# Gate products of the second block: half pieces, and two of the three branches' gates beside S5

## The chip, the cores and the metric

The kernel runs on one core of a Trainium2 chip. The metric is the device time of one execution in microseconds, the median of several runs. The core has five engines with a queue of instructions each: TensorE (PE in the profile), VectorE (DVE), ScalarE (ACT), GpSimd (POOL) and SyncE (SP, which here only starts transfers). Everything is float32.

## The reference, cut to what matters

The program computes two blocks in a row on x of 256 tokens by 1024. The change lies in the mixer of the second block. It projects its input with one wide matrix, runs three branches on parts of the projection (RWKV, attention, S5), and adds the branches up under gates:

```
def hybrid_mixer(x, w_in, ...):
    proj = x @ w_in
    y_a = rwkv7_mixer(proj[..., :OFF_MOBA], ...)
    y_b = moba_attention(heads(q), heads(k), heads(v))          # q, k, v: proj[..., OFF_MOBA:OFF_SSM]
    y_c = s5_mixer(proj[..., OFF_SSM:OFF_GATE], ...)
    gates = jax.nn.sigmoid(proj[..., OFF_GATE:] + gate_b).reshape(Bsz, L, N_BRANCHES, D_MODEL)
    merged = (gates[..., 0, :] * (y_a @ w_up_rwkv)
              + gates[..., 1, :] * (y_b @ w_up_moba)
              + gates[..., 2, :] * (y_c @ w_up_ssm))
    return merged @ w_out
```

D_MODEL is 1024, so the gates are a product of x with 1024 x 3072 weights, 1024 columns for each branch. The RWKV scan is y_t = S_t r_t with S_t = S_(t-1) (diag(w_t) + a_t b_t') + v_t k_t', eight heads of 64. S5 is a complex diagonal recurrence over the 256 tokens in 32 groups of 64 states, then a gelu and a gated linear unit:

```
    y = gelu(Re(C h) + d * u)        # h_t = lam * h_(t-1) + B u_t, complex
    zg = y @ glu_w + glu_b
    return zg[..., :D_SSM] * jax.nn.sigmoid(zg[..., D_SSM:])
```

## The kernel before, in words

**Order by steps.** Each engine has one queue, and its order is written by generators. A generator yields STEP (L28) where another may come in. `weave` (L149) goes round: one step of each generator, in the order given, then again. For the second block TensorE and ScalarE weave three generators (L3645, L3661): the RWKV branch, the "side" branches (input projections, attention, S5) and `gates_ahead`; VectorE weaves the first two (L3678). In this text a round is one turn of the weave, counted from 0; in a round an engine issues first the step of RWKV, then that of the side, then that of the gates. The rounds of the engines are not synchronised; semaphores make an engine wait where it needs another's result, and whatever stands behind in its queue waits with it.

**What the rounds hold on TensorE.** Rounds 0 to 12 are the 13 units of the input projection. RWKV's scan goes in two halves of 128 tokens, rounds 13 to 42 and 43 to 72, each of them: four transposes (rounds 13 to 16, 43 to 46), the products G and N1 of two heads a round (17 to 20, 47 to 50), a round of VectorE alone in which it makes the "first powers" (21, 51), then powers and partial inverses of the matrices of all heads (n0, p, Z, X, M: 22 to 30, 52 to 60), AK, G12, and R2 with Y0 (31 to 33, 61 to 63), four rounds of step and gain (34 to 37, 64 to 67), four of the chain over chunks (38 to 41, 68 to 71), and y (42, 72). After it come RWKV's normalisation and its up product. On the side, rounds 13 to 26 are attention, 27 and 28 its up product (`add_branch_tensor`, branch 1), 29 and 30 the input of S5, 33 its transposes. S5 then has 8 parts: `in` of part p + 1 in round 36 + 3p, `out` of part p in round 37 + 3p; rounds 59 and 60 are its gated unit.

**The gates.** One piece is 256 of the columns: 1 MB of weights in a slot of the ring of four slots (`WeightRing`, L111; SyncE loads piece n + 4 once piece n is used), and 32 matmuls of 128x128 by 256 columns into one bank (`product_cols`, L272, called by `gates_tensor`, L2095). Then `gates_scalar` (L2107) applies bias and sigmoid in two instructions. A branch has four pieces. `gates_ahead` (L3109) does branch 1 (attention) in rounds 13 to 16, one piece a round, and branch 0 (RWKV) in rounds 17, 20, 23 and 26. Its bank is bank 7 alone. Branch 2 (S5) is not ahead: `side_branches_tensor` (L3062) does its four pieces in rounds 61 to 64, after S5, and its up product in rounds 65 and 66.

**S5 on the other engines.** For part p VectorE turns the inputs by the angles ("a", L3000 to L3007) in round 34 + 3p, scans in 35 + 3p and turns back ("h", L3019 to L3024) in 36 + 3p. It needs the sine and cosine of the part: GpSimd reduces the angle (L2800, L2802), and ScalarE computes both in round 34 + 3p (`s5_sincos_scalar`, L2891: four instructions, L2894 to L2899). The functions of ScalarE lie in tables; where the next function is in another one, ScalarE loads it (ACT_TABLE_LOAD).

**Memory.** `rwkv_memory` (L2156) gives RWKV its tiles: among them b and k, which TensorE last reads for G and N1 of the second half of the scan (round 50), and bend and kend. The gates of S5 have a tile of their own in the memory of S5.

Of the kernel before, what the change touches and what calls it, by code (L numbers as in the profile page):

```python
# [15 lines left out]
P = 128  # L16
SEQ = 256
TT = SEQ // P
D = 1024
KT = D // P  # L20
# [7 lines left out]
STEP = "step"  # L28
# [1848 lines left out]
HEADS = 8  # L1877
# [215 lines left out]


def gates_tensor(c, s, pe, banks, branch, spaces=0):  # L2095
    for n in range(4):
        name = "gates", branch, n
        c.ring.next(name, s.pieces["gate"][branch][n])
        yield from c.ring.wait_ge(pe, name)
        bank = yield from banks.take(pe, *name)  # L2100
        product_cols(pe, bank, c.hT, c.ring.view(name), KT).then_inc(*pe.mark(*name))
        pe.also("used", *name)
        for _ in range(1 + spaces):
            yield STEP


def gates_scalar(c, s, act, banks, branch, gates, spaces=0):  # L2107
    for n in range(4):
        yield from act.wait_ge("gates", branch, n)
        src = as_cols(banks.of("gates", branch, n))  # L2110
        for j in range(2):
            f = 8 * branch + 2 * n + j
            ins = act.e.activation(gates[:, 2 * n + j, :], src[:, j, :], ACT.Sigmoid, bias=s.v["gate_b_2"][:, f:f + 1])  # L2113
        ins.then_inc(*act.mark("read", "gates", branch, n))
        for _ in range(1 + spaces):
            yield STEP
# [39 lines left out]
def rwkv_memory(s, mem):  # L2156
    s.rwkv_gates = mem.new("rwkv_gates", 8, SEQ)
    s.gates_at = mem.at - 8 * SEQ
    s.rw_yT = mem.new("rw_yT", 4, SEQ)
    s.rw_gate, s.bonus = mem.new("rw_gate", 4, SEQ), mem.new("rw_bonus", 4, SEQ)  # L2160
    s.AR = mem.new("rw_AR", 4, TT, 2 * P)
    s.b, s.k, s.bend, s.kend = (mem.new(f"rw_{name}", 4, SEQ) for name in ("b", "k", "bend", "kend"))
    s.bk_at = mem.at - 16 * SEQ
    s.chunk_decay, s.v_cols = mem.new("rw_chunk_decay", 4, N_CHUNK), mem.new("rw_v_cols", 4, SEQ)
    inner = mem.part()
    scan_memory(s, mem)
    s.lora_w, s.g2, s.z = inner.new("rw_lora_w", 512), inner.new("rw_g2", 512), inner.new("rw_z", 14, SEQ + 1)
    s.rw_r, s.rw_k = inner.new("rw_r", 4, SEQ), inner.new("rw_k_in", 4, SEQ)
    s.low, s.gate_in, s.shift_tmp = inner.new("rw_low", SEQ), inner.new("rw_gate_in", SEQ), inner.new("rw_shift", SEQ)
    s.logw, s.icl = inner.new("rw_logw", 4, SEQ), inner.new("rw_icl", 4, SEQ)  # L2170
    s.kk, s.rw_work, s.ka = inner.new("rw_kk", 4, SEQ), inner.new("rw_work", 4, SEQ), inner.new("rw_ka", 4, SEQ)
    s.run = inner.new("rw_run", 4, SEQ)
# [467 lines left out]
def rwkv_output_vector(c, s):  # L2640
    dve, banks, work, yT = c.rw.dve, c.rw_banks, flat_work(s), s.rw_yT
# [26 lines left out]
    dve.wait_own()  # L2668
    dve.e.tensor_tensor(yT, yT, s.rw_gate, MULT).then_inc(*dve.mark("branch", 0))
    yield STEP  # L2670
    yield from add_branch_vector(c, s, dve, banks, 0, 2, s.rwkv_gates, s.b[:, 0:2, :])

# [80 lines left out]
def s5_memory(s, mem):  # L2755
# [11 lines left out]
    s.sincos = [own, [s.chunk_start[:, n * 2 * SEQ:(n + 1) * 2 * SEQ].rearrange("p (j s) -> p j s", j=2) for n in range(2)]]  # L2767
    s.s5_angle = s.distance
    s.glu = [mem.new(f"s5_glu{n}", 4, SEQ) for n in range(2)]
    s.s5_gates, s.s5_tmp = mem.new("s5_gates", 8, SEQ), mem.new("s5_tmp", 2, SEQ)  # L2770


def s5_u_tensor(c, s):
# [288 lines left out]
def side_branches_tensor(c, s):  # L3062
    pe, banks = c.side.pe, c.side_banks
    yield from units_tensor(c, s)
    for h0 in (0, 4):
        yield from moba_tensor(c, s, h0)
    yield from add_branch_tensor(c, s, pe, banks, 1, s.mb_yT)
    yield from meet(c, "tensor", "moba", "side")
    yield from s5_u_tensor(c, s)
    yield from s5_tensor(c, s)  # L3070
    yield from gates_tensor(c, s, pe, banks, 2)
    yield from add_branch_tensor(c, s, pe, banks, 2, s.s5_yT)


def side_branches_scalar(c, s):
    act, banks = c.side.act, c.side_banks
    yield from units_scalar(c, s)
    for h0 in (0, 4):
        yield from moba_scalar(c, s, h0)
    for half in range(2):  # L3080
        yield STEP
    yield from meet(c, "scalar", "moba", "side")
    yield from s5_u_scalar(c, s)
    yield from s5_scalar(c, s)
    yield from act.wait_ge("branch", 2)
    yield from gates_scalar(c, s, act, banks, 2, s.s5_gates)
    for half in range(2):
        yield STEP


def side_branches_vector(c, s):
    dve, banks = c.side.dve, c.side_banks
# [5 lines left out]
    for n in range(2):  # L3098
        yield STEP
    yield from s5_vector(c, s)  # L3100
    for n in range(4):
        yield STEP
    yield from add_branch_vector(c, s, dve, banks, 2, 1, s.s5_gates, s.s5_tmp)


AHEAD_STEPS = 13


def gates_ahead_tensor(c, s):  # L3109
    for _ in range(AHEAD_STEPS):  # L3110
        yield STEP
    for branch, spaces in ((1, 0), (0, 2)):
        yield from gates_tensor(c, s, c.ahead.pe, c.ahead_banks, branch, spaces)


def gates_ahead_scalar(c, s):
    for _ in range(AHEAD_STEPS):
        yield STEP
    for branch, gates, spaces in ((1, s.merged, 0), (0, s.rwkv_gates, 2)):
        yield from gates_scalar(c, s, c.ahead.act, c.ahead_banks, branch, gates, spaces)  # L3120


# [690 lines left out]
```

## Time and profile before

| | us |
|---|---|
| median of 3 runs | 1790.57 |
| the runs | 1790.54, 1790.57, 1796.24 |
| the profiled execution's own time | 1796.08 |
| its span, first to last instruction | 1794.8 |
| TensorE, busy share of the span | 86% |
| VectorE | 56% |
| ScalarE | 43% |
| GpSimd | 13% |
| mean granted TensorE clock | 0.90 |

The span is cut by the page into 40 slices of 44.9 us. The second block's mixer, of which this document speaks, lies from about 860 us to 1395 us. The granted clock is the share of TensorE's full speed: 1.0 is 2.4 GHz and 0.5 is 1.2 GHz, and a value between them is a stretch in which it was at both. A busy share counts an instruction as busy for as long as it took, so at the half clock TensorE looks as busy with half the work.

### The profile page before, as it was taken

What the parts mean: (1) busy time and instruction counts of PE and PEld (TensorE: products, weight loads), DVE (VectorE), ACT (ScalarE), POOL (GpSimd) and SP (SyncE); (2) the same over time, 40 slices, a digit from 0 to 9 for tenths busy, and PEclk for the clock granted to TensorE, in tenths of its full rate; (3) what the DMA queues carried; (4) which work ended last, traced back from release to release, by engine and by line L of the source; (5) the groups of instructions that cost most, each with busy time, mean ns of one, the idle gap of its engine ahead of it and who ended that gap; (6) DMA issues with size and microseconds to landing.
All of it is one profiled execution on the core that took longest, in us unless ns stands there. A gap on an engine that the chain in (4) does not pass through costs nothing. (4 is left out here: it accounts for less than half of the span.)

```text
span 1794.8 us, 21644 instructions
## 1 busy us (share of the span) xinstructions
PE 1541.8 (86%) x8851; PEld 1288.1 (72%) x8851; DVE 1007.2 (56%) x1254; ACT 779.9 (43%) x1137; POOL 226.7 (13%) x337
## 2 busy tenths in 40 slices
PE   2979779997978879998979897788959589999996
PEld 1968669996877769997878786457848466666664
DVE  6557456666564344445473515984153666666665
ACT  3455255445454344444442222323100276666662
POOL 5421100001132000001880001220001000000000
PEclk9897789999887889999999997679969599999998
DMA  9745158776571046554433231001312369999882
GB/s 341 257 180 179 58 187 294 265 256 210 155 263 38 1 165 197 188 189 131 153 110 104 69 106 48 1 0 45 105 41 74 144 234 349 344 339 348 341 313 94
DMA packets 134585, 310.32 MB, mean 173 GB/s; under 512 B 6239, under 2 KB 99766, under 8 KB 114902
## 3 DMA queue, kind: packets, MB, share of 16 engines
q1 hardware_dynamic: 130326, 299.18, 47.1%
q0 software_dynamic: 3584, 8.71, 1.9%
q8 instruction: 70, 1.15, 0.3%
q10 hardware_dynamic: 576, 1.05, 0.2%
q14 instruction: 29, 0.24, 0.0%
HBM read 307.87 MB, written 1.05 MB: 172 GB/s over the span
## 5 line engine op out<-in xcount | busy, mean ns | idle before, releaser
L310 DVE TENSOR_TENSOR mlp_weights_lo<-weights,mlp_weights_hi 128x2048 fp32r<-128x2048 f32 x64 | 146.5, 2291 | 68.4 <-ACT mlp_weights_hi L300 67.5
L251 PE MATMUL bank<-mlp_in_hi,mlp_weights_hi 128*128 128x256 f32 x512 | 147.3, 288 | 10.3 <-DVE mlp_in_lo L694 10.3
L3501 DVE TENSOR_TENSOR expert_pair_lo<-weights,expert_pair_hi 128x2048 fp32r<-128x2048 f32 x53 | 119.9, 2290 | 63.9 <-ACT expert_pair_hi L3492 63.9
L252 PE MATMUL bank<-mlp_in_lo,mlp_weights_hi 128*128 128x256 f32 x512 | 147.0, 287 | 0.0
L253 PE MATMUL bank<-mlp_in_hi,mlp_weights_lo 128*128 128x256 f32 x512 | 147.0, 287 | 0.0
L300 ACT ACTIVATE mlp_weights_hi<-weights 128x2048 fp32r<-128x2048 f32 x64 | 121.9, 1908 | 55.9 <-issue 46.6
L251 PE MATMUL bank<-expert_pair_hi,x_block_hi 128*128 128x512 f32 x280 | 113.9, 407 | 5.2 <-issue 5.2
L253 PE MATMUL bank<-expert_pair_hi,x_block_lo 128*128 128x512 f32 x280 | 110.2, 394 | 0.0
L252 PE MATMUL bank<-expert_pair_lo,x_block_hi 128*128 128x512 f32 x280 | 110.2, 394 | 0.0
L251 PEld LDWEIGHTS bank<-mlp_in_hi,mlp_weights_hi 128*128 128x128 f32 x512 | 100.5, 196 | 12.1 <-issue 11.1
L562 DVE SCALAR_TENSOR_TENSOR ada<-weights,cond,ada 128x2048 f32<-128x2048 f32 x42 | 100.0, 2380 | 2.3 <-DMA weights<-in_w_ada 1.6
L252 PEld LDWEIGHTS bank<-mlp_in_lo,mlp_weights_hi 128*128 128x128 f32 x512 | 100.4, 196 | 1.1
L275 PE MATMUL bank<-hT,weights 128*128 128x256 f32 x448 | 100.0, 381 | 0.7 <-ACT merged L2113 0.6
L253 PEld LDWEIGHTS bank<-mlp_in_hi,mlp_weights_lo 128*128 128x128 f32 x512 | 100.4, 196 | 0.0
L251 PE MATMUL bank<-mlp_weights_hi,hidden_hi 128*128 128x512 f32 x256 | 100.0, 391 | 0.0
L252 PE MATMUL bank<-mlp_weights_lo,hidden_hi 128*128 128x512 f32 x256 | 100.0, 390 | 0.0
L253 PE MATMUL bank<-mlp_weights_hi,hidden_lo 128*128 128x512 f32 x256 | 99.6, 389 | 0.0
L3492 ACT ACTIVATE expert_pair_hi<-weights 128x2048 fp32r<-128x2048 f32 x53 | 99.2, 1907 | 0.0
L275 PEld LDWEIGHTS bank<-hT,weights 128*128 128x128 f32 x448 | 84.0, 190 | 13.4 <-issue 2.2
L1266 DVE TENSOR_TENSOR hidden_lo<-mlp_raw,hidden_hi 128x512 fp32r<-128x512 f32 x32 | 22.1, 692 | 96.8 <-ACT hidden_hi L1245 96.8
L3609 DVE TENSOR_TENSOR y_sorted<-bank,y_sorted 128x512 f32 (+1 forms) x70 | 48.4, 692 | 43.4 <-PE bank L3537 41.5
L1239 ACT ACTIVATE mlp_raw<-bank 128x512 f32<-128x512 f32 x32 | 19.1, 597 | 122.2 <-PE bank L253 122.2
(738 smaller groups left out, 3858.7 us busy)
## 6 DMA issues: line engine op xcount, KB each, us to landing
weights<-in_w_ada SPq DMA_DIRECT2D x48, 1024.0 KB, 5.0
weights<-in_w_in SPq DMA_DIRECT2D x45, 1024.0 KB, 5.1
weights<-in_expert_w_gate SPq DMA_DIRECT2D x35, 1024.0 KB, 4.8
weights<-in_w_up SPq DMA_DIRECT2D x32, 1024.0 KB, 5.5
weights<-in_w_down SPq DMA_DIRECT2D x32, 1024.0 KB, 5.1
weights<-in_expert_w_up SPq DMA_DIRECT2D x18, 1024.0 KB, 6.1
weights<-in_expert_w_down SPq DMA_DIRECT2D x18, 1024.0 KB, 6.7
expert_raw<-in_expert_w_up SPq DMA_DIRECT2D x17, 1024.0 KB, 6.0
```

Source lines behind the costliest of these rows:

```text
L251: pe.e.matmul(out, lhsT[0], rhs[0], start=start, stop=False)
L252: pe.e.matmul(out, lhsT[0], rhs[1], start=False, stop=False)
L253: return pe.e.matmul(out, lhsT[1], rhs[0], start=False, stop=stop)
L275: ins = pe.e.matmul(bank[:, j * SEQ:(j + 1) * SEQ], w[:, k, j * P:(j + 1) * P], xT[:, k, :], start=k == 0, stop=k == tiles - 1)
L300: act.e.activation(self.of(n)[0], ring.view(name), ACT.Copy).then_inc(*act.mark(*self.key, "high", n))
L310: dve.e.tensor_tensor(lo, ring.view(name), hi.bitcast(F32), SUB).then_inc(*dve.mark(*self.key, "low", n))
L562: dve.e.scalar_tensor_tensor(part, ring.view(name), s.cond[:, k:k + 1], part, MULT, ADD).then_inc(*dve.mark(*name))
L1239: act.e.activation(s.raw, as_cols(c.up_banks.of("up", l, n)), ACT.Relu).then_inc(*act.mark("read", "up", l, n))
L1266: dve.e.tensor_tensor(lo, s.raw, hi.bitcast(F32), SUB).then_inc(*dve.mark("hidden low", l, n))
L3492: act.e.activation(pair[0][:, :, i * D_EXPERT:(i + 1) * D_EXPERT], expert_raw(s, kind, n), ACT.Copy).then_inc(*act.mark("expert", "high", ...
L3501: dve.e.tensor_tensor(pair[1][:, :, part], expert_raw(s, kind, n), pair[0][:, :, part].bitcast(F32), SUB).then_inc(*dve.mark("expert", "lo ...
L3609: dve.e.tensor_tensor(part, c.banks[4 + 2 * (n % 2) + half].unsqueeze(1), part, ADD).then_inc(*dve.mark("expert", "added", n, half))
```

## The change

Three things change, besides blank lines. A gate piece on TensorE is two steps of 16 matmuls, with a STEP between them; ScalarE's step for the piece starts with a STEP, so that it stands in the round of the second half. The gates of all three branches are ahead: AHEAD gives for each branch the empty steps before it and the empty steps behind each piece. By the rounds above that is branch 1 in rounds 13 to 20, two rounds a piece without a gap; branch 0 in rounds 35 and 36, 38 and 39, 41 and 42, 44 and 45; and branch 2 in rounds 51 and 52, 54 and 55, 57 and 58, 60 and 61. The sigmoids stand in the second round of each pair, behind the side's step of that round. The four pieces in rounds 61 to 64 of the side generator go, so S5's up product is in rounds 61 and 62 on TensorE and in 60 and 61 on VectorE. And the gates of S5 are written over RWKV's b and k, so ScalarE waits for the last N1 product before them (`"scan", 1, "N1", 7`), and RWKV's up product takes bend, not b, as its work tile.

```diff
--- before.py
+++ after.py
@@ -2093,12 +2093,19 @@
 
 
 def gates_tensor(c, s, pe, banks, branch, spaces=0):
+
     for n in range(4):
         name = "gates", branch, n
         c.ring.next(name, s.pieces["gate"][branch][n])
         yield from c.ring.wait_ge(pe, name)
-        bank = yield from banks.take(pe, *name)
-        product_cols(pe, bank, c.hT, c.ring.view(name), KT).then_inc(*pe.mark(*name))
+        bank, w = (yield from banks.take(pe, *name)), c.ring.view(name)
+        for j in range(2):
+            for k in range(KT):
+                ins = pe.e.matmul(bank[:, j * SEQ:(j + 1) * SEQ], w[:, k, j * P:(j + 1) * P], c.hT[:, k, :], start=k == 0,
+                                  stop=k == KT - 1)
+            if j == 0:
+                yield STEP
+        ins.then_inc(*pe.mark(*name))
         pe.also("used", *name)
         for _ in range(1 + spaces):
             yield STEP
@@ -2106,6 +2113,7 @@
 
 def gates_scalar(c, s, act, banks, branch, gates, spaces=0):
     for n in range(4):
+        yield STEP
         yield from act.wait_ge("gates", branch, n)
         src = as_cols(banks.of("gates", branch, n))
         for j in range(2):
@@ -2159,7 +2167,9 @@
     s.rw_yT = mem.new("rw_yT", 4, SEQ)
     s.rw_gate, s.bonus = mem.new("rw_gate", 4, SEQ), mem.new("rw_bonus", 4, SEQ)
     s.AR = mem.new("rw_AR", 4, TT, 2 * P)
-    s.b, s.k, s.bend, s.kend = (mem.new(f"rw_{name}", 4, SEQ) for name in ("b", "k", "bend", "kend"))
+    bk = mem.new("rw_bk", 8, SEQ)
+    s.b, s.k, s.s5_gates = bk[:, 0:4, :], bk[:, 4:8, :], bk
+    s.bend, s.kend = mem.new("rw_bend", 4, SEQ), mem.new("rw_kend", 4, SEQ)
     s.bk_at = mem.at - 16 * SEQ
     s.chunk_decay, s.v_cols = mem.new("rw_chunk_decay", 4, N_CHUNK), mem.new("rw_v_cols", 4, SEQ)
     inner = mem.part()
@@ -2668,7 +2678,7 @@
     dve.wait_own()
     dve.e.tensor_tensor(yT, yT, s.rw_gate, MULT).then_inc(*dve.mark("branch", 0))
     yield STEP
-    yield from add_branch_vector(c, s, dve, banks, 0, 2, s.rwkv_gates, s.b[:, 0:2, :])
+    yield from add_branch_vector(c, s, dve, banks, 0, 2, s.rwkv_gates, s.bend[:, 0:2, :])
 
 
 
@@ -2767,7 +2777,7 @@
     s.sincos = [own, [s.chunk_start[:, n * 2 * SEQ:(n + 1) * 2 * SEQ].rearrange("p (j s) -> p j s", j=2) for n in range(2)]]
     s.s5_angle = s.distance
     s.glu = [mem.new(f"s5_glu{n}", 4, SEQ) for n in range(2)]
-    s.s5_gates, s.s5_tmp = mem.new("s5_gates", 8, SEQ), mem.new("s5_tmp", 2, SEQ)
+    s.s5_tmp = mem.new("s5_tmp", 2, SEQ)
 
 
 def s5_u_tensor(c, s):
@@ -3068,7 +3078,6 @@
     yield from meet(c, "tensor", "moba", "side")
     yield from s5_u_tensor(c, s)
     yield from s5_tensor(c, s)
-    yield from gates_tensor(c, s, pe, banks, 2)
     yield from add_branch_tensor(c, s, pe, banks, 2, s.s5_yT)
 
 
@@ -3082,8 +3091,6 @@
     yield from meet(c, "scalar", "moba", "side")
     yield from s5_u_scalar(c, s)
     yield from s5_scalar(c, s)
-    yield from act.wait_ge("branch", 2)
-    yield from gates_scalar(c, s, act, banks, 2, s.s5_gates)
     for half in range(2):
         yield STEP
 
@@ -3098,25 +3105,26 @@
     for n in range(2):
         yield STEP
     yield from s5_vector(c, s)
-    for n in range(4):
-        yield STEP
     yield from add_branch_vector(c, s, dve, banks, 2, 1, s.s5_gates, s.s5_tmp)
 
 
-AHEAD_STEPS = 13
+AHEAD = (1, 13, 0), (0, 14, 1), (2, 4, 1)
 
 
 def gates_ahead_tensor(c, s):
-    for _ in range(AHEAD_STEPS):
-        yield STEP
-    for branch, spaces in ((1, 0), (0, 2)):
+    for branch, steps, spaces in AHEAD:
+        for _ in range(steps):
+            yield STEP
         yield from gates_tensor(c, s, c.ahead.pe, c.ahead_banks, branch, spaces)
 
 
 def gates_ahead_scalar(c, s):
-    for _ in range(AHEAD_STEPS):
-        yield STEP
-    for branch, gates, spaces in ((1, s.merged, 0), (0, s.rwkv_gates, 2)):
+
+    for (branch, steps, spaces), gates in zip(AHEAD, (s.merged, s.rwkv_gates, s.s5_gates)):
+        for _ in range(steps):
+            yield STEP
+        if branch == 2:
+            yield from c.ahead.act.wait_ge("scan", 1, "N1", HEADS - 1)
         yield from gates_scalar(c, s, c.ahead.act, c.ahead_banks, branch, gates, spaces)
```

## Rows read from the trace of the kernel before

**Rows 1.** The page, part 2: granted TensorE clock in tenths, 40 slices.

```profile
PEclk9897789999887889999999997679969599999998
```

**Rows 2.** Windows: busy us (and instructions) of each engine, clock, DMA share, GB/s.

```profile
952.20:1051.30 99.10, 90.31 (x536) 79.03 (x537) 35.60 (x77) 32.64 (x69) 0.00 (x0) 0.98 0.23 75
...
1105.30:1171.30 66.00, 52.79 (x410) 33.29 (x409) 52.05 (x84) 22.21 (x42) 19.66 (x12) 0.66 0.00 1
1171.30:1196.40 25.10, 18.05 (x82) 12.26 (x81) 23.43 (x41) 1.67 (x4) 3.19 (x2) 0.77 0.00 1
1196.40:1234.85 38.45, 34.63 (x208) 26.58 (x209) 26.25 (x41) 15.07 (x24) 3.33 (x2) 0.84 0.00 1
...
1253.90:1310.90 57.00, 53.52 (x451) 46.61 (x450) 12.60 (x22) 6.82 (x15) 0.00 (x0) 1.00 0.36 121
```

**Rows 3.** TensorE in order of time, rounds 13 to 26: start us, us, what.

```profile
953.44 7.17 PE L275 MATMUL bank<-hT,weights 128*128 128x256 f32 x32
...
1012.44 2.05 PE L2357 MATMUL bank<-scan_N,scan_PP 128*128 128x128 f32 x16
1017.36 0.98 PE L1307 MATMUL bank<-identity,mb_scores 128*128 128x128 f32 x4 [2.87 <-DVE mb_scores L2742]
1018.13 3.31 PE L2357 MATMUL bank<-scan_PP,scan_N 128*128 128x128 f32 x16
...
1039.78 1.09 PE L1307 MATMUL bank<-identity,mb_scores 128*128 128x128 f32 x8 [3.02 <-DVE mb_scores L2742]
```

**Rows 4.** VectorE in order of time, rounds 20 and 21.

```profile
1004.19 0.69 DVE L2544 TENSOR_TENSOR scan_G<-bank,pair_masks 128x512 f32<-128x512 f32 x1 [0.37 <-PE bank L2387]
...
1011.17 1.22 DVE L2559 TENSOR_TENSOR scan_N<-scan_N,scan_N 128x1024 f32<-128x1024 f32 x1
```

**Rows 5.** Waits from 1100 to 1240 us: who for whom, total us, times, longest.

```profile
DVE s_br L3000 <- ACT s_cos L2899: 11.9, 2, 7.5
...
PE bank L2856 <- DVE s_gi L3024: 11.7, 4, 3.9
```

**Rows 6.** TensorE in order of time, beside S5 (in of parts 1, 4; out of 6).

```profile
1116.14 4.20 PE L2822 MATMUL bank<-s_u,s_bT 32*128 32x256 f32 x8 [1.37 <-DVE s_gi L3001]
...
1159.52 2.31 PE L2822 MATMUL bank<-s_u,s_bT 32*128 32x256 f32 x8
...
1216.97 0.62 PE L2856 MATMUL bank<-s_br,s_cT 128*32 128x256 f32 x2
...
1219.71 2.05 PE L2357 MATMUL bank<-scan_N,scan_PP 128*128 128x128 f32 x16
```

**Rows 7.** ScalarE in order of time: gate, table load, exp; sine and cosine of part 1.

```profile
1012.50 0.84 ACT L2113 ACTIVATE rwkv_gates<-bank,columns 128x256 f32<-128x256 f32 x2 [12.32 <-PE bank L275]
1013.36 1.28 ACT L1294 ACT_TABLE_LOAD   x1
1014.65 0.40 ACT L1294 ACTIVATE mb_scores<-mb_scores,mb_negmax 128x128 f32<-128x128 f32 x1
...
1124.56 0.62 ACT L2894 ACTIVATE chunk_start<-distance 128x512 f32<-128x512 f32 x1
...
1126.39 0.72 ACT L2899 ACTIVATE chunk_start<-chunk_start,ones 128x512 f32<-128x512 f32 x1
```

**Rows 8.** VectorE in order of time: turns of parts 0 and 4, first G of round 47.

```profile
1114.80 0.69 DVE L3000 TENSOR_TENSOR s_br<-bank,s_cos 128x512 f32<-128x512 f32 x1 [7.50 <-ACT s_cos L2899]
...
1166.58 0.68 DVE L3000 TENSOR_TENSOR s_br<-bank,s_cos 128x512 f32<-128x512 f32 x1
...
1172.53 0.69 DVE L2544 TENSOR_TENSOR scan_G<-bank,pair_masks 128x512 f32<-128x512 f32 x1 [1.89 <-PE bank L2387]
```

**Rows 9.** TensorE in order of time: rounds 52, 60 and 68.

```profile
1196.38 3.75 PE L2357 MATMUL bank<-scan_N,scan_PP 128*128 128x128 f32 x16 [6.36 <-DVE scan_N L2559]
...
1243.43 1.80 PE L2357 MATMUL bank<-scan_N,scan_P 128*128 128x128 f32 x14 [1.51 <-ACT scan_N L2364]
...
1310.88 1.80 PE L2471 MATMUL bank<-scan_state,scan_N 128*128 128x64 f32 x8 [1.49 <-DVE scan_N L2595]
```

## The prediction

> **What bounds the kernel now.** I read the clock of the page first, then the windows of the mixer, then each engine in order of time, and the list of waits to see who holds whom.
>
> The clock row [rows 1] shows slices at 6 and 7 in the middle of the second block. The windows [rows 2] say what lies there. From 952 to 1051 us (rounds 13 to 26: attention, the scan's first half, eight gate pieces) TensorE is busy 90 of 99 us at a clock of 0.98, VectorE 36 and ScalarE 33: TensorE sets the pace. From 1105 to 1171 us (rounds 34 to 46: S5's parts 0 to 3) it is the other way round: VectorE is busy 52 of 66 us, TensorE 53, but at a clock of 0.66, so its work would take 52.8 x 0.66 = 35 us at full clock. From 1171 to 1196 us VectorE is busy 23.4 of 25.1. From 1196 to 1235 us TensorE's 34.6 at 0.84 are 29 us of full-clock work in 38.5. From 1254 to 1311 us (rounds 61 to 67) TensorE is busy 53.5 of 57 at 1.00 again, VectorE 12.6, ScalarE 6.8. So TensorE is the limit before S5 and behind it, and has room beside S5: 66 - 35 = 31 us and 38.5 - 29 = 9.5 us, and a wait of 6.36 us at the end of the stretch between [rows 9].
>
> A gate piece takes 7.17 us at full clock, less what overlaps with its neighbours, 7.1 [rows 3], so a branch takes 28.4 and half a piece 3.55.
>
> **The change part by part.**
>
> *Branch 0 leaves rounds 17 to 26.* 4 x 7.1 = 28.4 us of TensorE go, and the halves of branch 1 fill rounds 13 to 20. What do the pieces cover there? Two waits for attention's maps stand in the rows, 2.87 and 3.02 us [rows 3]. I carried rounds 13 to 26 through with the pieces at their new places. The piece of round 20 covers the first powers: VectorE is done with them at 1012.4, which is 8.2 us after it took the first G of round 20 at 1004.2 [rows 4]. After the G of the round and the scores the new order has only a half piece there, 3.55 us in place of 7.1, so TensorE waits about 3.5 us for the powers. The wait of 2.87 shrinks by some 1.9, since the exponentials, too, have only waited for the powers, and ScalarE has no gate and no new table before them (it loaded one, 1.28 us, between gate and exp [rows 7]). The one of 3.02 shrinks by about 1, for the same reason. Sum of the waits: +3.5 - 1.9 - 1 = about +0.5. More waits in a row can let the clock fall: after the wait of 2.87 us the next 16 matmuls took 3.31 us, where 16 of the same form took 2.05 before it [rows 3]. I allow two such falls, about 2 us. Stage: -28.4 + 0.5 + 2 = **-26**. Bounds: -28.4 (waits all hidden), and -14, if half of what goes comes back as waits; VectorE and ScalarE are each busy a third of the stage, so I take the value near the first end.
>
> *Branch 0 goes into rounds 35 to 45.* Eight halves are 28.4 us at full clock; with TensorE's 35 that is 63.4, in a stage of 66. So at full clock it just fits, and the price is what order and clock add. The clock: the stage starts low (in of part 1 takes 4.20 us, that of part 4 takes 2.31 [rows 6]), so the first half piece takes 7.1 and the work beside it also doubles: +5 or so. Then TensorE has no gap left and I expect 1.0, as it is wherever gates run [rows 2]. The order: ScalarE's sigmoid of a piece stands right before sine and cosine of the next part. It waits for the second half, takes 0.84, loads the sine's table 1.28 and computes for 2.55 (1124.56 to 1127.11) [rows 7]: VectorE can start the next part 4.7 us after the half piece ends. For parts 1 to 3 that is no later than TensorE itself comes to the part's out. For part 4 it binds. The last half ends when TensorE has done 35 - 3 (out of part 3, 2.7 us at full clock [rows 6], is behind it) + 28.4 + 5 = 65 us, plus about 3 us of waits for VectorE, which it has today (11.7 us in four waits for S5 [rows 5]); that is 1105.3 + 68 = 1173. Part 4 starts at 1178, against 1166.6 [rows 8]: +11.5. VectorE's next G stood behind a wait of 1.89 us for TensorE [rows 8], which some of it absorbs, or not, if TensorE is late as well. I take **+12**. Bounds: 0 (all in the room of 31 us) and +28.4 (nothing hidden at full clock); beyond it only by the clock, a rival below.
>
> On tables the Trainium skill speaks against this edit: in "ScalarE: Activation LUTs", section "What ACT_TABLE_LOAD costs", a switch of tables costs about 1.28 us for the load and 1.38 more for a drain. By that page the sum would be 1.4 us worse for each of some six parts, 8 us. The rows show the load of 1.28 us begin 0.02 us after the sigmoid and the exponential begin 0.01 us after the load [rows 7], so this trace shows no drain, and the sum has none.
>
> *Rounds 47 to 51.* No piece in them but the first half of branch 2. VectorE is the limit (23.4 of 25.1 us): the 12 us are carried through, neither grown nor made good. The half piece stands in round 51, where TensorE waits 6.36 us for the powers [rows 9], and costs nothing; without that cover it costs 3.55. ScalarE's new wait for the last N1 is for a product a round back. Behind it in its queue stands the evacuation of n0, which comes later anyway.
>
> *Rounds 52 to 68.* Five more halves (branch 2, pieces 0 to 2) come beside parts 5 to 7: 17.75 us with TensorE's 29 make 46.9 in a stage of 38.45: **+8.4**. Here TensorE binds. The sigmoid of piece 2 stands behind ScalarE's evacuation of the gated unit and before that of M, so Z3 waits not 1.51 us [rows 9] but one load and one sigmoid more: **+2**. The last two halves stand in rounds 60 and 61: **+7.1**. The four pieces of rounds 61 to 64 go: **-28.4** (the stage's clock is 1.00). S5's up product moves from rounds 65, 66 to 61, 62 and costs the same; there it covers the evacuation of G12, now about 2 us of wait: **-2**. In rounds 64 to 67 step and gain lose their cover; the wait of 1.49 us behind them [rows 9] stands already, and VectorE's work in the whole stage is 12.6 us [rows 2], so between 0 and a few us can come out there, and I take 0. VectorE's product for S5's up stands in round 60, before its copy of AK, on which G12 waits; but a half piece of 3.55 us lies between on TensorE, longer than the two VectorE instructions and the copy. The clock falls once more, at the half piece and n0 after the powers: +2. Stage: 8.4 + 2 + 7.1 - 28.4 - 2 + 2 = **-11**. Bounds: -21 (the five halves hidden) and +2 (halves at 1.2 GHz).
>
> *What costs nothing.* b, k and bend share the memory of before, so no address conflict or copy is added. The ring's loads keep their number; each still has four pieces of lead, and the DMA share in S5 is 0.00 [rows 2]. Behind round 68 nothing changes.
>
> **Sum.** -26 + 12 - 11 = -25 us against the profiled execution's 1796.1 (span 1794.8 and 1.3 around it): 1771. That execution was at the upper of the values shown; the median is 1790.6, 0.997 of it, so 1771.1 x 0.997 = **1765.7**.
>
> **Rivals.**
>
> *The coupling through ScalarE and VectorE is longer than I think* (chance 0.26, with the case that attention's waits come out in rounds 17 to 26). S5's parts today follow one another on VectorE every (1166.6 - 1114.8) / 4 = 13 us [rows 8]. I have TensorE at 16 us a part; if out, sigmoid, table, sine and turn in series make it 18, four parts cost 20 us, not 12, and three more in the next stage 4 more: -13 in all, 1777.5. The other case has -14 for the first stage: also about 1777. For: 11.9 us of waits for the cosine stand there already, with no gate before it [rows 5]. Against: ScalarE is busy 22 of 66 us.
>
> *The clock stays low beside S5* (0.08): the other side. If the half pieces between S5's narrow matmuls don't raise it, the stage takes 63.4 / clock. At 0.66, as now, that is 96 us, +30, and the next stage 46.9 / 0.84, +17: the sum is -26 + 30 - 11 + 9 = +2, 1792.6. At 0.55 the stage takes 115, +49: 1811. It decides from a clock of about 0.67 in the stage down. For: the clock there is 0.66 with TensorE busy 80% of the time. Against: wherever gate pieces run it is 0.98 to 1.00 [rows 2].
>
> *It doesn't matter* (0.03): the 31 us of room fall short and the 28.4 taken from either side return as waits. It needs both stages wrong at once.
>
> **How the numbers follow.** My forecast has 0.63, its own spread 1757 to 1774. The range goes to the long coupling and a bit beyond, 1753 to 1784. A measurement of this kernel can tell about 0.3% (5 us) from no change. Faster: 0.63 + 0.26 = 0.89; same 0.03; slower 0.08.
>
> **What would show it.** After the change attention's last heads product should end about 26 us earlier, with a wait of some 3.5 us before n0 of the first half. Beside S5's parts 0 to 3 the clock should be above 0.85, the stage 76 to 80 us, and TensorE's waits for S5's turns nearly gone. Sine and cosine of parts 1 to 4 should follow a table load right behind a sigmoid. Rounds 61 to 67 should take about 30 us: today's 57 less four pieces and the wait of 2, plus one half piece. I am wrong if the clock beside S5 stays under 0.7, if VectorE's waits for the cosine grow past 15 us, or if rounds 13 to 26 shorten by less than 20 us.

## The result, and the profile after

| | before | after |
|---|---|---|
| median, us (5 runs each) | 1790.57 | 1782.10 |
| lowest and highest | 1790.46, 1796.24 | 1777.96, 1783.53 |
| after / before, 95% interval | | 0.9943 [0.9929, 0.9956] |
| the profiled execution: time, span | 1796.08, 1794.8 | 1780.62, 1779.4 |
| granted clock, mean | 0.90 | 0.908 |

The change makes the kernel 0.57% faster, 10 us by the ratio, where 25 were forecast. The measured time lies in the range, near its upper end, and by the rival of the long coupling (1777.5), not by the forecast (1765.7).

I cut the second block's mixer by landmarks that both traces have, from the first instruction of round 13 on. "Turn" is VectorE's start on a part of S5, as in [rows 8].

| stretch, us | before | after | difference | forecast |
|---|---|---|---|---|
| round 13 to attention's up product | 100.9 | 73.3 | -27.6 | -26 |
| to the turn of part 0 | 61.7 | 62.4 | +0.7 | 0 |
| to the turn of part 4 | 51.8 | 76.0 | **+24.2** | +12 |
| to n0 of the second half | 29.8 | 31.8 | +2.0 | 0 |
| to the last product of round 68 | 114.5 | 101.7 | -12.8 | -11 |
| to the RWKV branch's up product | 36.4 | 37.7 | +1.3 | 0 |
| sum | 395.0 | 383.0 | -12.1 | -25 |

A forecast of 0 stands where the prediction named no change.

"The last product of round 68" is the group of [rows 9] at 1310.88 us, and a stretch ends where its landmark starts. Four of the terms are near. One is off by 12 us, and it is nearly all of the miss. Round 13 itself starts 2.4 us earlier (at 949.84 in place of 952.23 us), before anything that was changed. The two profiled executions differ by 15.5 us, the ratio of all runs says 10: that of before was the slow end of its runs. So differences below 5 us between executions are read from stages, not from totals.

The windows of the changed kernel answer to [rows 2]: rounds 13 to 26; S5's parts 0 to 3 by TensorE's rounds 34 to 46; rounds 47 to 51; rounds 52 to 60; rounds 61 to 67. The last row goes from the turn of part 0 to that of part 4.

```profile
949.84:1021.25 71.41, 61.17 (x409) 52.70 (x409) 34.88 (x76) 23.71 (x58) 0.00 (x0) 1.00 0.19 60
1075.30:1162.04 86.74, 81.56 (x537) 60.55 (x536) 50.57 (x79) 33.96 (x55) 16.28 (x10) 0.80 0.15 49
1162.04:1193.43 31.39, 25.45 (x98) 17.37 (x97) 27.82 (x47) 3.88 (x8) 6.43 (x4) 0.73 0.00 1
1193.43:1239.85 46.42, 45.70 (x289) 37.83 (x289) 26.64 (x41) 20.60 (x31) 3.22 (x2) 1.00 0.16 47
1260.98:1295.10 34.12, 34.12 (x370) 31.07 (x368) 14.22 (x23) 4.02 (x9) 0.00 (x0) 0.95 0.39 124
...
1085.58:1161.61 76.03, 70.96 (x430) 52.45 (x429) 49.29 (x77) 29.03 (x46) 13.08 (x8) 0.83 0.17 56
```

Beside S5 the clock rose from 0.66 to 0.80, less than the 0.85 I wanted. VectorE's work in the stretch hardly changed (50.6 us, 52.1 before), but the stretch grew by 20.7: VectorE is idle for 36 us of it, where it was for 14. The waits of 1075 to 1193 us say for whom (engine, line, waited for: total us, times, longest). They answer to [rows 5], from VectorE's side:

```profile
DVE s_br L3010 <- ACT s_cos L2909: 13.5, 3, 8.3
DVE s_br L3010 <- ACT chunk_start L2909: 10.3, 2, 5.9
DVE scan_N L2611 <- PE bank L2481: 7.1, 1, 7.1
...
ACT rwkv_gates L2121 <- PE bank L2104: 37.8, 4, 15.1
```

The cosine lies in s_cos and chunk_start by turns. The turns waited 23.8 us for it, 8.3 of them ahead of part 0 (7.5 before, [rows 8]) and 15.5 in the stretch between parts 0 and 4, where before had 0.85. ScalarE itself is idle: it waits 37.8 us for half pieces of TensorE. In order of time on ScalarE, round 39:

```profile
1125.09 0.84 ACT L2121 ACTIVATE rwkv_gates<-bank,columns 128x256 f32<-128x256 f32 x2 [15.06 <-PE bank L2104]
1125.94 1.28 ACT L2904 ACT_TABLE_LOAD   x1
1127.24 0.63 ACT L2904 ACTIVATE s_sin<-distance 128x512 f32<-128x512 f32 x1
...
1129.08 0.72 ACT L2909 ACTIVATE s_cos<-s_cos,ones 128x512 f32<-128x512 f32 x1
```

ScalarE had nothing to do for 15 us, while sine and cosine of part 2 stood in its queue behind a sigmoid that waited for TensorE. GpSimd, which prepares their argument, had been idle since 1113.1 (the window of 1113.10 in the last fence of this document). At 1129.8 us VectorE's turn of part 2 begins, 3.48 us after it could. The same on TensorE, three of the eight half pieces:

```profile
1080.34 4.20 PE L2832 MATMUL bank<-s_u,s_bT 32*128 32x256 f32 x8
1084.60 6.51 PE L2104 MATMUL bank<-hT,weights 128*128 128x256 f32 x16
...
1118.36 6.69 PE L2104 MATMUL bank<-hT,weights 128*128 128x256 f32 x16
...
1129.50 3.67 PE L2104 MATMUL bank<-hT,weights 128*128 128x256 f32 x16
```

A half piece takes 3.67 us at a clock of 1.0 and 6.5 to 6.7 at the low level. The eight take 39.3 us together (6.51, 5.96, 3.67, 6.69, 3.67, 5.41, 3.62, 3.72), where I had 28.4 + 5.

### The profile page after: what moved, and what is told of

Same layout as the page of the kernel before. It is cut to its first block and busy times, and to the rows that moved or that the text cites. A ratio compares the mean times of both kernels' runs of the same rounds, so it can differ in the third digit from the quotient of the medians.

```text
span 1779.4 us, 21643 instructions
## 1 busy us (share of the span) xinstructions
PE 1537.1 (86%) x8851; PEld 1285.2 (72%) x8851; DVE 1010.1 (57%) x1254; ACT 786.7 (44%) x1142; POOL 226.4 (13%) x337
## 5 line engine op out<-in xcount | busy, mean ns | idle before, releaser
L251 PE MATMUL bank<-mlp_in_hi,mlp_weights_hi 128*128 128x256 f32 x512 | 147.4, 288 | 10.3 <-DVE mlp_in_lo L694 10.3
L251 PEld LDWEIGHTS bank<-mlp_in_hi,mlp_weights_hi 128*128 128x128 f32 x512 | 100.5, 196 | 12.1 <-issue 11.1
L2104 PEld LDWEIGHTS bank<-hT,weights 128*128 128x128 f32 x384 | 78.0, 208 | 18.7 <-PE bank L2832 4.2
```

Of the source, the lines that this page charges most:

```text
L251: pe.e.matmul(out, lhsT[0], rhs[0], start=start, stop=False)
L2104: ins = pe.e.matmul(bank[:, j * SEQ:(j + 1) * SEQ], w[:, k, j * P:(j + 1) * P], c.hT[:, k, :], start=k == 0, stop=k == KT - 1)
```

## The experiments

Theory A, from these rows: the order on ScalarE. What stands there ahead of sine and cosine and waits for TensorE holds them; they hold VectorE's turn, and that holds the rest. Theory B: the volume. The half pieces at a low clock are simply too much beside S5; the order matters little. Each experiment is an edit of the changed kernel; the ratios are to the kernel before, run beside it. They were run in three sets, in which the kernel before took 1793.69 us (e1 to e4), 1795.67 (e5 to e8) and 1795.88 (e9 to e12), so the medians of two sets don't compare directly, while the times in the expectations start from the first measurement, with 1790.57. The stretches are the better scale: where nothing differs they agree to 0.1 us (the first is 73.3 us in ten of the traces).

| run | median us | ratio, 95% interval | parts 0 to 4, us | round 13 to up product |
|---|---|---|---|---|
| before | 1793.69 to 1795.88 | 1 | 51.8 | 395.0 |
| changed | 1782.10 | 0.9943 [0.9929, 0.9956] | 76.0 | 383.0 |
| e1_sine_first | 1771.24 | 0.9889 [0.9866, 0.9911] | 71.1 | 376.2 |
| e2_no_table | 1772.76 | 0.9878 [0.9855, 0.9902] | 68.1 | 372.9 |
| e3_branch2_only | 1774.68 | 0.9897 [0.9877, 0.9918] | 51.8 | 376.4 |
| e4_branch0_only | 1789.33 | 0.9984 [0.9967, 1.0001] | 72.8 | 388.0 |
| e5_half_volume | 1772.80 | 0.9876 [0.9858, 0.9894] | 67.2 | 373.5 |
| e6_first_piece_ahead | 1766.65 | 0.9837 [0.9817, 0.9857] | 67.5 | 369.4 |
| e7_branch2_earlier | 1770.04 | 0.9871 [0.9853, 0.9888] | 71.1 | 371.1 |
| e8_places_by_waits | 1752.38 | 0.9767 [0.9748, 0.9785] | 51.7 | 353.2 |
| e9_sines_earlier | 1766.74 | 0.9850 [0.9832, 0.9868] | 64.6 | 369.4 |
| e10_sines_earlier_half_volume | 1756.92 | 0.9790 [0.9772, 0.9809] | 56.9 | 359.3 |
| e11_places_sines_earlier | 1754.84 | 0.9777 [0.9761, 0.9794] | 51.0 | 353.0 |
| e12_whole_pieces | 1790.99 | 0.9977 [0.9965, 0.9989] | 88.7 | 393.5 |

**e1: sine before sigmoid.** ScalarE takes each sigmoid of branch 0 one round later; those of branch 2 keep their rounds.

```
 for _ in range(steps):
->
 for _ in range(steps + (0, 1, -1)[(1, 0, 2).index(branch)]):
```

> ScalarE's sigmoids of branch 0 stand one round later, behind the sine and cosine of the next part; TensorE and VectorE keep their order. In the changed kernel VectorE's parts 0 to 4 of S5 start 19.0 us apart, and it waits 4.4, 3.5, 5.9 and 1.8 us for the cosine of parts 1 to 4. Theory A (the sigmoid in front of the sine holds VectorE, and the low clock comes from the waits that this makes): the four waits go, parts are about 16 us apart, the clock of the stage (rounds 34 to 46) rises from 0.80 to 0.9 or more, time 1770 to 1774 us where the changed kernel has 1782. Theory B (half pieces between narrow products run at the low clock by themselves, and TensorE is what VectorE waits for in the end): the waits for the cosine turn into waits for TensorE's products, parts stay at 18 us or more, the clock at 0.8, time 1779 to 1783.

Measured: 4.9 us of the 24 come back, and the time is in Theory A's range (1771.24), but the parts are 17.8 us apart, near Theory B's 18. VectorE's waits for the cosine of parts 1 to 4 were 4.4, 3.5, 5.9 and 1.8 us and are 2.8, 0, 10.0 and 0: two are gone, and one has grown. ScalarE around the sine of part 3, and the turn behind it:

```profile
1138.03 0.60 ACT L2504 ACTIVATE scan_W<-bank 128x512 f32<-128x512 f32 x1 [18.19 <-PE bank L2390]
1138.64 1.28 ACT L2904 ACT_TABLE_LOAD   x1
```

```profile
1142.53 0.69 DVE L3010 TENSOR_TENSOR s_br<-bank,chunk_start 128x512 f32<-128x512 f32 x1 [10.03 <-ACT chunk_start L2909]
```

The sigmoid is out of the way, but the scan's own evacuation of scan_W stands there too, and waits for transposes that TensorE does behind a half piece. The queue has two such gatekeepers. So this run moved only one, and doesn't decide.

**e2: no table.** The gates of branch 0 are linear (the sigmoid is left out), so ScalarE changes tables less.

```
 ACT.Sigmoid  ->  ACT.Identity if branch == 0 else ACT.Sigmoid
```

> Branch 0's gates are computed without the sigmoid (bias only), so ScalarE loads no table for them and none for the sine behind them; the order is that of the changed kernel. Theory A: only the wait for the half piece counts, of the 4.7 us between it and VectorE's start 1.3 go, so about 4 x 1.3 = 5 us, 1777. Theory B: nothing, 1780 to 1783. Theory C (the tables are the greater part of the miss): 8 us or more, under 1774.

Measured: 7.9 us less between parts 0 and 4 and 1772.8 us, about what I had set for Theory C (8 us or more, under 1774). Four loads lie between a half piece and a turn there, 5.1 us at 1.28; that more came back is for TensorE's side, which is busy 65.8 us in place of 71.0, at a clock of 0.89. 16 us stay, so the loads are a part of the price and not all of it.

**e3, e4: one branch alone.** In e3 branch 0 stands ahead of S5, in rounds 21 to 31; in e4 branch 2 is four whole pieces in rounds 61 to 64 again.

```
 AHEAD = (1, 13, 0), (0, 14, 1), (2, 4, 1)
->
 AHEAD = (1, 13, 0), (0, 0, 1), (2, 18, 1)     # e3
 AHEAD = (1, 13, 0), (0, 14, 1)                # e4, and in the tail:
+    yield from whole_gates_tensor(c, s, pe, banks, 2)
```

> Branch 2's gates stay in rounds 51 to 61 as in the changed kernel, branch 0's go back before S5, as half pieces in rounds 21 and 22, 24 and 25, 27 and 28, 30 and 31. Against the kernel before this is the move of branch 2 alone. By the trace of the changed kernel rounds 52 to 67 give 12.8 us and the first 35 rounds nothing: 1778 to 1780. If the two moves of the change work against each other (branch 0 beside S5 delays the rest), it is better than the changed kernel, if branch 0's move is worth something by itself, worse: Theory A and B both say that branch 0's move gave 27.7 and cost 27.0, so the same as the changed kernel within 3 us.

> Branch 0's gates beside S5 as in the changed kernel, branch 2's as four whole pieces in rounds 61 to 64 as in the kernel before. This is the move of branch 0 alone. By the two traces it gives 27.7 us in rounds 13 to 26 and costs 20.7 in rounds 34 to 46 and 6.3 in rounds 47 to 51: 1790 us, the same as before. Had my forecast been right it would be 1790.6 - 26 + 12 = 1777.

Measured: in e3 S5 is back at 51.8 us, to the tenth what it was; the stretches ahead of it take 82.9 and 72.8 us in place of 73.3 and 62.4, 20.0 more, so by the stages branch 0's move from there into S5 costs 24.2 and saves 20.0. Left ahead of S5, it makes the kernel faster than the change does (0.9897 against 0.9943; the intervals don't meet), where I had expected 1778 to 1780 us, about the same. In e4 the stretch behind n0 takes 113.5 us in place of 101.7: the move of branch 2 is worth 11.8, and I had 11. Branch 0's move alone can't be told from no change (0.9984, an interval that reaches 1): the gain of the change is branch 2's.

**e5: half of the volume.** The RWKV branch's gates sum four of their eight k-tiles; the other half of their products is left out.

```
+ tiles = KT // 2 if branch == 0 else KT
- for k in range(KT):
+ for k in range(tiles):
```

> Every half piece of branch 0 sums over four of the eight tiles of 128 rows only: 8 matmuls in place of 16, same places, same waits, same sigmoids. In the changed kernel VectorE's parts 0 to 4 take 76.0 us (51.8 before). Theory A (the order on ScalarE is what costs): the tables and the order are all there, so of the 24.3 us some 15 or more stay, 1773 to 1776. Theory B (the volume of matmuls beside S5, at a clock that is half the time the low one, makes TensorE late for everything behind it): TensorE has 14 us less at full clock and 20 or more at the clocks seen, so under 10 of the 24.3 us stay, under 1769.

Measured: 14.2 us of work at full clock go, and 8.8 us come back; 15.4 of the 24.2 stay with half of the work. By the volume alone half of the price, 12.1, should have gone with half of the work. 8.8 is less, but not by so much that the volume could be left out. What stays is what I had set for Theory A (15 or more).

**e6, e7: small moves on top of e1.** e6 puts the first piece of branch 0 into rounds 31 and 32, e7 starts branch 2 one round earlier.

```
 (0, 0, 31, 32, 32)          # e6: branch, piece, rounds of its halves, round of the sigmoid
 (2, 4, 1) -> (2, 3, 1)      # e7
```

> As e1_sine_first, but piece 0 of branch 0 is in rounds 31 and 32, in front of the 8 us in which TensorE waits for VectorE to make S5's matrices. Theory B: the piece costs nothing there, and rounds 35 and 36 lose a half piece each that took 6.5 and 3.7 us: parts 0 to 4 take 71.1 - 8 to 10 = 61 to 63 us, time 1763. If the wait of 8 us does not swallow the piece (because ScalarE's table and sigmoid come in the way of S5's start) it is 1768 to 1770.

> As e1_sine_first, but branch 2's pieces start one round earlier, in round 50: the last half piece but one comes between the gated unit's product and Z3, and the sigmoid of piece 2 no longer stands between ScalarE's evacuation of the gated unit and that of M. In the changed kernel TensorE waits 3.66 us there and does Z3's products at the low clock (3.65 us, 1.95 at the full one). If that is what it costs, 1771 - 5 = 1766; if the wait only moves to another place, 1769 to 1772.

Measured: e6 takes 3.6 us off S5 and 2.9 off the stretch ahead of it, where TensorE waits 7.9 us for VectorE's matrices of S5, so the piece there adds nothing. One gate piece less beside S5 is worth that little, because a wait for chunk_start stays (8.3 us); I had expected 61 to 63 us for the parts and got 67.5. e7 gains 8.3 us between n0 and round 68, loses 0.6 behind them and 2.7 ahead of n0, against e1, 5.1 in sum; the ratios of the two don't part.

**e9, e10: the order mended.** Sine and cosine of parts 1 to 7 stand one round earlier on ScalarE, ahead of both gatekeepers; e10 has half of branch 0's volume as well.

```
 yield from s5_sincos_scalar(c, s, act, part)
 yield STEP
+if part:
+    yield STEP
 if part + 1 < 8:
     yield from s5_angles_scalar(s, act, part + 1)
 yield STEP
-yield STEP
...
+yield STEP        # behind the loop over the parts
```

> The changed kernel; sine and cosine of S5's parts 1 to 7 stand one round earlier on ScalarE: ahead of the sigmoid of the round and of the scan's evacuation, both of which wait for TensorE. Places and volume of the pieces are untouched. Theory A (the order on ScalarE: what waits there for TensorE holds sine and cosine, these hold VectorE, and the waits that follow lower the clock): VectorE's waits for cosine and chunk_start (24 us between parts 0 and 4) nearly go, parts 0 to 4 take 60 to 66 us where they took 76.0, time 1766 to 1770 us. Theory B (the volume of the half pieces at a low clock; the order matters little): parts 0 to 4 stay at 72 us or more, time 1778 or more.

> As the run before, and the RWKV branch's gates sum only four of their eight k-tiles (half of their products is left out, 14 us at full clock), so that this pair gives the price of the volume alone once ScalarE's order is out of the way. Theory A: parts 0 to 4 take 52 to 56 us, near the 51.8 of the kernel before. Theory B: the pair differs by 12 us or more, as the halves at the low clock cost most, and parts 0 to 4 take 60 or more.

Measured: 64.6 us between the turns, 11.4 less, and 1766.7 us, both as Theory A had them. (The 24 us of waits in the expectation count the one ahead of part 0; between the parts there were 15.5.) VectorE's waits in e9 (1070 to 1175 us), and the window from turn 0 to turn 4:

```profile
DVE s_br L3012 <- ACT s_cos L2909: 8.3, 1, 8.3
DVE scan_N L2611 <- PE bank L2481: 6.2, 2, 5.4
```

```profile
1079.90:1144.50 64.60, 64.14 (x419) 48.56 (x418) 47.97 (x76) 27.48 (x45) 13.94 (x8) 0.89 0.16 50
```

Only the one wait ahead of part 0 is left, no turn of parts 1 to 4 waits for ScalarE, and what VectorE waits for is TensorE. TensorE is busy 64.1 of 64.6 us: with the order mended it is the limit, as the prediction had it, and the clock of 0.89 is what it still pays. The pair e9 and e10 prices the volume: 14.2 us of full-clock work cost 7.7 us (expected 12 or more by B, and 52 to 56 us for the stretch by A: it took 56.9, just over). The last member of the row is e11 below, which has the sines of e9 and no piece of branch 0 between these turns: 51.0 us. So the 24.2 us come apart as 11.4 for the order (e9), 7.7 for one half of the volume (e10) and 5.9 for what is left of the pieces, less the 0.8 by which e11 is under the kernel before. The 5.9 are the other half of the products with their sigmoids and table loads, and no run parts these.

How the order reaches TensorE can be read off the windows. It is idle for 5.1 of 76.0 us in the changed kernel and for 0.5 of 64.6 in e9: 4.6 of the 11.4 us. The other 6.8 us it is busy, at a clock of 0.83 and of 0.89; some 1.6 of them are products of part 3's `out` that e9 does behind turn 4.

**e12: whole pieces.** One part of the change undone: branch 0 in whole pieces at the places of the second halves, the sigmoids where they were.

```
 (0, n, 36 + 3 * n, 36 + 3 * n, 36 + 3 * n)   for n in 0 to 3
```

> The changed kernel with the RWKV branch's pieces whole again, in rounds 36, 39, 42 and 45, at the places of the second halves; the sigmoids stand where they stood. One part of the change undone: the halving in S5. Theory A: the sigmoid ends at the same place of the queue, and TensorE does the same work; within 3 us of the changed kernel's 1782. If the halving itself is what makes room (a whole piece of 7.1 us at full clock, 13 at the low one, in one turn), parts 0 to 4 take 82 us or more and the time is 1788 or more.

Measured: 88.7 us and 1791, so my expectation failed. TensorE does the same work and the pieces don't even take longer in sum (9.82, 9.89, some 8.5, 10.10 us: 38.3, where the halves took 39.3). What grew is the waits. VectorE's in e12 from 1070 to 1175 us:

```profile
DVE scan_N L2611 <- PE bank L2481: 11.2, 1, 11.2
...
DVE scan_v L2547 <- PE bank L2390: 6.3, 1, 6.3
```

and TensorE's own waits between the same parts (10.3 us):

```profile
PE bank L2481 <- DVE scan_N L2611: 5.8, 1, 5.8
PE bank L2832 <- DVE s_gr L3014: 4.5, 2, 3.7
```

TensorE and VectorE hand the scan's products back and forth. A whole piece of 10 us between two of them makes VectorE wait, and the work that VectorE is then late with makes TensorE wait in turn. By the windows from turn 0 to turn 4 TensorE is idle for 10.8 us (5.1 in the changed kernel) and busy for 77.9 at a clock of 0.78 (71.0 at 0.83). The halving of branch 0's pieces is worth 12.7 us of the stretch; with them whole the change as it stands would be worth 0.2% (I tried them at the places of the second halves alone).

**e8, e11: the version that came of it.** Pieces only where TensorE is the limit or waits anyway, none between the turns of S5's parts 0 and 4: rounds 21 to 24, 31 and 32 ahead of S5 (the wait of 7.9 us), and 72 to 75, beside the wait for VectorE ahead of the RWKV branch's up product. Branch 2 goes one round earlier. e11 has the sines of e9 as well.

```
PLACES = [(1, 0, 13, 14, 14), (1, 1, 15, 16, 16), (1, 2, 17, 18, 18), (1, 3, 19, 20, 20),
          (0, 0, 21, 24, 24), (0, 1, 31, 32, 32),
          (2, 0, 50, 51, 51), (2, 1, 53, 54, 54), (2, 2, 56, 57, 57), (2, 3, 59, 60, 60),
          (0, 2, 72, 73, 74), (0, 3, 74, 75, 75)]
```

> Half pieces only where TensorE waits anyway. Branch 0: piece 0 in rounds 21 (wait for the first powers) and 24, piece 1 in 31 and 32 (the 8 us before S5), pieces 2 and 3 in rounds 72 to 75, in the 14 us of wait for RWKV's normalisation, whose result alone needs these gates. Branch 2 in rounds 50 to 60. Beside S5's parts 0 to 4 stands nothing. By the stages of the traces, from round 13 to round 68: 73.3 + 1 (rounds 13 to 26), 62.5, 51.8 (parts 0 to 4, as before the change), 29.8, 100, in sum 318 us where the kernel before has 358.7 and the changed one 345.3; behind it nothing is added if the waits hold the pieces. So 40 us under before, 1751; if the two late pieces run at the low clock and come out, 1758. Theory A and B agree here; what it tests is the reading that the place, not the move, decides.

> The version with the places chosen by waits (1752.4 us, parts 0 to 4 in 51.7), and sine and cosine one round earlier as well. No half piece stands between S5's parts there, so Theory A expects little: the wait of 7 to 8 us for cosine that the kernel before had goes, but the transposes and the turn of the part set the pace; 1748 to 1753 us. If ScalarE's order holds S5 without gates too, parts 0 to 4 fall below 46 and the time below 1747.

Measured: 1752.4 us, by the ratios 2.3% less than before and 1.8% less than the changed kernel, and within 1.4 us of what was expected. Branch 0's pieces add 2.7 us to the first stretch (76.0, where the changed kernel has 73.3), take 2.8 off the second (59.6) and add 2.0 to the last (39.7), 1.9 us in sum, where beside S5 they cost 24.2. Two of TensorE's waits show why: the first fence has them in the changed kernel, ahead of S5 and ahead of the RWKV branch's up product, the second what e8 left of them. Then the window of e8 from turn 0 to turn 4.

```profile
PE bank L2846 <- DVE s_cc L2996: 7.9, 1, 7.9
...
PE bank L275 <- DVE rw_yT L2679: 13.7, 1, 13.7
```

```profile
PE bank L2846 <- DVE s_cc L2996: 3.0, 1, 3.0
...
PE bank L275 <- DVE rw_yT L2679: 6.8, 1, 6.8
```

```profile
1085.27:1136.94 51.67, 38.63 (x244) 23.64 (x243) 47.18 (x77) 15.98 (x31) 13.64 (x9) 0.67 0.00 1
```

Between S5's turns VectorE is busy 47.2 of 51.7 us: S5 runs at VectorE's pace, TensorE's clock is 0.67, and the 4.5 us in which VectorE is idle are the most that this can cost. e11 is the same within its interval and 0.7 us shorter between the turns, so without pieces the order on ScalarE costs next to nothing there.

## Why the prediction was right or wrong

*Branch 0 leaves rounds 17 to 26: right.* -26 forecast, -27.6 measured, near the bound of -28.4. The wait of 3.5 us for the powers ahead of n0 is there, at 3.42; the maps' waits shrank from 2.87 and 3.02 to 1.24 and 2.68. The clock stayed at 1.00 (n0 takes 2.05 us right behind the wait), so the two falls that I had allowed 2 us for didn't come.

```profile
999.88 2.05 PE L2367 MATMUL bank<-scan_N,scan_PP 128*128 128x128 f32 x16 [3.42 <-DVE scan_N L2569]
1003.17 0.66 PE L1307 MATMUL bank<-identity,mb_scores 128*128 128x128 f32 x4 [1.24 <-DVE mb_scores L2752]
...
1016.71 1.09 PE L1307 MATMUL bank<-identity,mb_scores 128*128 128x128 f32 x8 [2.68 <-DVE mb_scores L2752]
```

*Branch 0 goes into rounds 35 to 45: wrong, and this is the step that failed.* +12 forecast, +24.2 measured. The step had the right queue and the right latency: "VectorE can start the next part 4.7 us after the half piece ends". In round 39 the half piece's end releases the sigmoid at 1125.09 and the turn begins at 1129.83, 4.74 us later. What failed is the sentence behind it: "For parts 1 to 3 that is no later than TensorE itself comes to the part's out". I had compared the end of the sine with what TensorE does next. But the turn is VectorE's. It waited 4.4, 3.5, 5.9 and 1.8 us for the cosine of parts 1 to 4, and 12.4 us of VectorE's work stand behind the turn of part 2 in its queue (1129.83 to 1142.25); so every part pays, not only part 4. I summed engines' work (TensorE 63.4 us in 66) where the stretch is a loop through three in-order queues: half piece, sigmoid, table, sine, turn, products. Its length was 19.0 us a part (76.0 / 4); the rival that adds these in series had taken 18, without adding them up, and named 1777.5. e9 changed the order alone and gave back 11.4 us of the 12.2 that I missed (TensorE was idle for only 4.6 of these 11.4, as the windows under e9 say); e2, e5 and e12 each changed one member and each moved it.

*The clock in that step: a term too small.* +5 forecast for one half piece and its neighbours at the low level; four of the eight were there in whole or in part, for 39.3 us in place of 28.4, so about 11 for the pieces alone. With their neighbours it is more: in the stage TensorE is busy 81.6 us at 0.80, some 65 us of full-clock work (I had 63.4), so the low level takes about 16 us where I had 5. "Then TensorE has no gap left and I expect 1.0" is the second sentence that failed. The two are not independent, as the busy time shrinks when the order is mended (e9), but that it is the waits which lower the clock is not shown: e9 has a low stretch with no wait listed (last section). The rival with a clock under 0.67 didn't come: it is 0.80 in the stage. Between turns 0 and 4 it is 0.83, and 0.89 in e9, where the waits for ScalarE are gone.

*Rounds 47 to 51: wrong by a little.* From turn 4 to n0 +2.0 were measured, 0 forecast. The half piece of round 51 costs nothing, as said: TensorE's wait at n0 shrank from 6.36 [rows 9] to 2.49 us, and e3 and e9, which have the same half piece and the same wait, take 29.7 us for the stretch. What grew is on VectorE, which waits 3.1 us for the product G where it waited 2.1 and is busy 28.3 us in place of 27.4. Why is open.

*Rounds 52 to 68: right in sum.* -11 forecast, -12.8 measured; e4 gives 11.8 for it by itself. The wait of Z3 grew by 2.15 us (3.66, before 1.51), I had 2; rounds 61 to 67 take 34.1 us, I had about 30, and the row of rounds 52 to 60 makes it good with a clock of 1.00. TensorE's cover in rounds 64 to 67 wasn't missed: it is busy 34.12 of 34.12 us. My upper bound of +2 for the stage was too low for what I named with it: five halves at half speed add 17.75 us to -11, which is +5 or more.

*The table loads.* The forecast took 1.28 us and no drain. The rows after agree: in round 39 the sigmoid's record ends at 1125.93, the load begins at 1125.94 and the sine at 1127.24. The page "ScalarE: Activation LUTs" of the Trainium skill, section "What ACT_TABLE_LOAD costs", adds 1.38 us of drain to each switch of tables. No row here shows that. The loads cost more than I had for another reason, their place in the loop (e2: 7.9 us).

*What I had said would prove me wrong.* VectorE's waits for the cosine past 15 us: 13.5 for s_cos alone, 23.8 with chunk_start. The stage was to take 76 to 80 us at a clock over 0.85: 86.7 at 0.80. TensorE's waits for S5's turns were to be nearly gone, and they are (2.2 us in two, where [rows 5] have 11.7): it is VectorE that waits now, and I had not followed that side.

Open is what holds the clock down beside S5 where TensorE doesn't wait, and what makes up the 5.9 us between e10's stretch and e11's. The profiled execution of before was 5.5 us over its median; no stage of the mixer shows it. Over the profiled executions of all kernels round 13 begins between 943.97 us (e7) and 952.52 (e2), ahead of anything that differs; that of before has 952.23.

## What to carry to other kernels

Work put beside a chain that passes through several in-order queues is not free because each engine has room in it. Write down for each queue what the inserted instruction waits for and what stands behind it; if the chain's next step does, the wait can be paid in every turn of the loop (here four times, 15.5 us in all). First move whatever the chain needs ahead of the instructions that wait for inserted work (here a one-round shift of sine and cosine, 11.4 us); better still, put filler where an engine is already the limit or already waits: the list of its longest waits is the list of places to try (1.9 us for four pieces in e8). And keep one turn of the filler short: whole pieces cost 12.7 us more than halves.

## What the runs showed of the hardware

In these traces the clock doesn't follow the busy share alone. From 1080.30 to 1091.00 us of the changed kernel TensorE is busy 10.58 of 10.70 us, without a wait, at a clock of 0.53; from 1124.90 on it is busy as well, at 1.00:

```profile
1080.30:1091.00 10.70, 10.58 (x27) 7.24 (x24) 5.39 (x7) 3.56 (x7) 5.70 (x4) 0.53 0.00 0
1113.10:1124.90 11.80, 11.68 (x33) 8.52 (x34) 5.65 (x10) 0.00 (x0) 0.00 (x0) 0.57 0.01 1
1124.90:1133.10 8.20, 8.20 (x49) 6.03 (x48) 3.66 (x7) 6.81 (x10) 2.19 (x2) 1.00 0.42 128
```

The first stretch is S5's input product with 32 rows (4.20 us for 8 matmuls) and a half piece of full width behind it; before it came the scan's products with 32 rows and S5's transposes, and before these the wait of 7.9 us. From 1113.10 on, behind a wait of 2.31 us, it is much the same, 11.68 of 11.80 us at 0.57. I had expected that a half piece in such a place brings the clock back within itself; it ends at the low level, after 6.51 us.

It comes without a wait too. In e9 no wait of TensorE is listed from 1070 to 1150 us. A half piece at 1114.83 takes 3.67 us, the full level. Then come 5 us of the scan's narrow products and S5's input product, and the next half piece is at the low level:

```profile
1118.92 1.57 PE L2492 MATMUL bank<-scan_N,scan_N 64*64 64x32 f32 x48
1120.41 2.85 PE L2832 MATMUL bank<-s_u,s_bT 32*128 32x256 f32 x8
1123.32 6.45 PE L2104 MATMUL bank<-hT,weights 128*128 128x256 f32 x16
```

Gates raise the clock of a stage, from 0.66 to 0.80 here, but not to 1.00.
